# Strassen convolution: partial sums kept in the accumulators, weight sums formed once and stored, VectorE in GpSimd's place

## The chip, the cores and the metric

One core of a Trainium2 chip runs the whole program. The metric is the device time of one execution in microseconds (us). Of the core's engines, TensorE multiplies matrices into eight accumulator banks, VectorE and ScalarE work element by element and can reach those banks, GpSimd works element by element in local memory alone, and SyncE (SP) issues transfers.

## The reference

One decoder step on 2048 prompt tokens and 8 x 16 sample tokens, 2176 in all, 1024 features, fp32 throughout. The change touches only the input side of the first mixer:

```python
def _rmsnorm(x, g):
    y = xf * lax.rsqrt(jnp.mean(xf * xf, axis=-1, keepdims=True) + EPS)
    return (y * g.astype(jnp.float32)).astype(x.dtype)

def _short_conv_mixer(xn, prev, w_in, conv_w, w_out):
    proj = xn @ w_in                                   # 1024 x 4096
    b_gate, c_gate, h, z = jnp.split(proj, 4, axis=-1)
    u = c_gate * h
    up = jnp.concatenate([prev.astype(u.dtype), u], axis=1)
    conv = conv_w[0] * up[:, 0:T]
    for i in range(1, CONV_WIDTH):                     # width 3
        conv = conv + conv_w[i] * up[:, i:i + T]
    y = jax.nn.silu(z) * b_gate * conv
    return y @ w_out, up[:, T:]
...
x = x + _rmsnorm(h, a_norm_post[i])                    # then keys, values,
                                                       # attention, output
```

## The kernel before, in words

The program is a row of phases: convolution (0 to 812 us), output projection of that mixer, keys and values, attention, and the end. Each phase is a block in which every engine has its own instruction list, and the engines wait for each other by semaphores. The lists are written out by hand, so the order on each engine is fixed, and an instruction that waits holds up everything behind it on its engine.

`phase_conv` computes `xn @ w_in`, the gates, the convolution and y. It goes over the tokens in three passes (`PASSES`, line 219: 640, 768 and 768 tokens), each as two halves of 320 or 384 columns. Within a pass it goes over 16 strips: 8 blocks of 128 features (`c`), and for each two strips `m`, of which the first (even n) gives c_gate and h, the second (odd n) z and b_gate. n counts all 48 strips.

A strip is a 2 x 2 block product by the Strassen-Winograd scheme: seven products in place of eight (`A11_B11` to `A22_T4`, line 226). Weights are the A side, tokens the B side. Each product has an inner length of 512, which is 4 blocks of 128, and every fp32 operand is split into a high and a low part, with three matmuls per block (lines 474 to 476): 12 matmuls a product, 84 a strip. The high part is a ScalarE copy into the rounded type (`high_w` line 546, `high_x` line 535), the low part a VectorE subtraction (`low` line 695, `low_x` line 689). Four of the seven weight operands are sums S1 to S4 of quarters of the raw weights; GpSimd forms them for every strip of every pass (`sums`, line 810). Four of the seven token operands are differences T1 to T4, formed once a pass, on GpSimd but for two in pass 0 (`first_differences`, `second_difference`, `third_difference`, lines 827 to 846, and 753 to 758). There is one high and one low buffer for each of the seven operands, so a split for strip n+1 waits for the product of strip n.

Each strip has three accumulator banks, A, B and C, and strips alternate between two sets. Bank A holds P1 (A11 B11), ScalarE copies it out (line 630), and P2 is added to it by TensorE: c11. Bank B holds P5, VectorE adds P1 to it into v (line 770), P6 (S4 B22) is added to it by TensorE, and VectorE adds u2: c12 (lines 788 to 793). Bank C holds the S2 product; VectorE adds P1 into u2 (line 777); the S3 product is added by TensorE and VectorE adds v: c22 (`c22`, line 708); the A22 product is added and VectorE adds P1: c21 (`c21`, line 715). TensorE's order in strip n (lines 502 to 509): A11, S1, the A22 product of strip n-1, S2, A12, S4, S3.

From the four quarters GpSimd forms u = c_gate * h (`set_u`, line 848). ScalarE and VectorE apply the three taps (`keep_and_tap` line 579, `taps` line 721), GpSimd multiplies by silu(z) (`gate`, line 868) and by b_gate (`finish`, line 878), and SP stores y.

The token tiles of 128 rows are normalized: ScalarE squares and sums (`sums_of`), VectorE takes the reciprocal, ScalarE scales (`scale`), TensorE transposes (`turn`), VectorE multiplies by the gain into the stage (`stage`). The five tiles of pass 0 come first; the other twelve are spread over the odd strips, one tile to two strips, in the pass before they are used. Such a tile's scaling is the last ScalarE work of a strip, and its transposes are the first TensorE work of the next (lines 494 and 653). SP's order is in lines 395 to 446: raw weight blocks (512 KB each, two a strip), tiles, y.

## Time and profile before

| | us |
|---|---|
| median of three runs | 2836.79 (2834.07 to 2838.17) |
| profiled execution, its own time | 2833.93 |
| its span, first to last instruction | 2832.2 |
| TensorE busy | 2690.6 (95%) |
| VectorE busy | 1998.5 (71%) |
| ScalarE busy | 1606.5 (57%) |
| GpSimd busy | 1435.6 (51%) |
| mean granted TensorE clock | 0.98 of 2.4 GHz |

The span is the time from the first to the last instruction of the profiled execution; the execution's own time is 1.7 us longer. The table sums all phases. The change concerns the first 812 us, so the views below look at this stretch. In the trace, idle time of an engine is put down to the instruction that released it ("<-"). A matmul's duration is longer than the distance to the next one, as matmuls overlap in the array: for the pace of TensorE one reads the starts.

### The profile page before, as it was taken

To read this page: it belongs to the slowest core of one execution; us is meant where nothing else is said; L and a number is where in the kernel's file an instruction comes from. 1 tells how busy PE (TensorE), PEld (TensorE's weight loads), DVE (VectorE), ACT (ScalarE), POOL (GpSimd) and SP (SyncE) were. 2 spreads that over 40 slices of the span, in tenths; PEclk is the share of its full clock that TensorE was granted. 3 is DMA by queue.
4 is the path that set the end of the run, shared out by engine and by line. 5 is a ranking of instruction groups with operands and counts; after the bars stand their busy time and mean duration, and the time that the engine had idled before them with its cause. 6 is when DMAs were issued, how large, how long until landed. Compare 5 with 4: busy or idle time off the path is not lost. (4 is left out here: it accounts for less than half of the span.)

```text
span 2832.2 us, 44315 instructions
## 1 busy us (share of the span) xinstructions
PE 2690.6 (95%) x15048; PEld 2407.0 (85%) x15048; DVE 1998.5 (71%) x2590; ACT 1606.5 (57%) x3224; POOL 1435.6 (51%) x1251
## 2 busy tenths in 40 slices
PE   5997999799899999999989999999999999989998
PEld 5997999799888888889978988888888888877886
DVE  6777766877754460102248999999999999998775
ACT  5564454444333441111147888888888888875543
POOL 5767655776540021003346777777786768652110
PEclk8998999899999999999999999999999999999999
DMA  3332232133244443434578777767676866757873
GB/s 107 118 99 69 85 110 83 51 113 94 71 146 133 131 147 136 178 114 154 164 218 251 216 230 228 207 216 232 196 242 204 244 208 196 234 180 214 245 227 108
DMA packets 371536, 467.40 MB, mean 165 GB/s; under 512 B 53346, under 2 KB 312546, under 8 KB 365316
## 3 DMA queue, kind: packets, MB, share of 16 engines
q1 hardware_dynamic: 364612, 440.69, 51.4%
q0 software_dynamic: 6720, 24.13, 2.6%
q8 instruction: 110, 1.80, 0.3%
q14 instruction: 94, 0.77, 0.1%
HBM read 340.95 MB, written 123.81 MB: 164 GB/s over the span
## 5 line engine op out<-in xcount | busy, mean ns | idle before, releaser
L2318 POOL TENSOR_TENSOR a_a<-a_a,a_prod 128x512 f32<-128x512 f32 (+3 forms) x640 | 662.0, 1052 | 274.1 <-DVE a_prod L2269 196.9
L474 PE MATMUL c_pc<-c_xh,c_wh 128*128 128x384 f32 (+1 forms) x1344 | 453.3, 337 | 58.3 <-DVE c_sums L706 32.8
L2269 DVE TENSOR_TENSOR_SCAN a_prod<-a_keep,a_prod,a_restart 128x513 f32<-128x513 f32 x384 | 478.4, 1270 | 7.6 <-ACT a_keep L2213 7.0
L476 PE MATMUL c_pc<-c_xh,c_wl 128*128 128x384 f32 (+1 forms) x1344 | 449.2, 334 | 0.0
L475 PE MATMUL c_pc<-c_xl,c_wh 128*128 128x384 f32 (+1 forms) x1344 | 449.2, 334 | 0.0
L2212 ACT ACTIVATE a_a<-a_pz 128x512 f32<-128x512 f32 (+3 forms) x640 | 357.4, 559 | 70.2 <-PE a_pz L2139 48.5
L2279 DVE TENSOR_TENSOR a_atl<-a_pt,a_ath 128x512 fp32r<-128x512 f32 (+3 forms) x640 | 363.4, 600 | 31.9 <-ACT a_ath L2222 28.9
L2222 ACT ACTIVATE a_ath<-a_pt 128x512 fp32r<-128x512 f32 (+3 forms) x640 | 332.9, 559 | 56.9 <-PE a_po L2153 33.3
L2213 ACT ACTIVATE a_keep<-a_pz 128x512 f32<-128x512 f32 (+3 forms) x640 | 361.2, 565 | 0.0
L474 PEld LDWEIGHTS c_pc<-c_xh,c_wh 128*128 128x128 f32 x1344 | 261.5, 195 | 63.9 <-DVE c_sums L706 35.9
L2162 PEld LDWEIGHTS a_pt<-ident_r,a_bits 128*128 128x128 f32 x2176 | 231.0, 141 | 52.1 <-DVE a_atl L2279 8.4
L475 PEld LDWEIGHTS c_pc<-c_xl,c_wh 128*128 128x128 f32 x1344 | 261.3, 194 | 0.0
L476 PEld LDWEIGHTS c_pc<-c_xh,c_wl 128*128 128x128 f32 x1344 | 261.0, 194 | 0.0
L2138 PE MATMUL a_pz<-a_kh,a_q 128*128 128x512 f32 (+3 forms) x640 | 247.5, 390 | 8.5 <-ACT a_keep L2213 6.1
L2151 PE MATMUL a_po<-a_ath,a_v 128*128 128x512 f32 (+3 forms) x640 | 250.0, 394 | 1.9 <-POOL a_v L2329 1.1
L2162 PE MATMUL a_pt<-ident_r,a_bits 128*128 128x128 f32 x2176 | 243.9, 241 | 7.3 <-DVE a_atl L2279 5.0
L699 DVE TENSOR_TENSOR c_wl<-c_s,c_wh 128x512 fp32r<-128x512 f32 x192 | 199.2, 1037 | 69.9 <-ACT c_wh L554 65.1
L2139 PE MATMUL a_pz<-a_kl,a_q 128*128 128x512 f32 (+3 forms) x640 | 234.2, 368 | 0.0
L2153 PE MATMUL a_po<-a_atl,a_v 128*128 128x512 f32 (+3 forms) x640 | 229.3, 367 | 0.0
L554 ACT ACTIVATE c_wh<-c_s 128x512 fp32r<-128x512 f32 x192 | 120.5, 629 | 176.3 <-PE c_pc L476 138.3
L699 DVE TENSOR_TENSOR c_wl<-c_raw,c_wh 128x512 fp32r<-128x512 f32 x144 | 152.7, 1060 | 94.0 <-ACT c_wh L554 92.3
L2263 DVE TENSOR_TENSOR_SCAN a_prod<-a_keep,a_restart 128x128 f32<-128x128 f32 (+3 forms) x256 | 197.3, 807 | 9.5 <-ACT a_keep L2213 8.8
(252 smaller groups left out, 5999.6 us busy)
## 6 DMA issues: line engine op xcount, KB each, us to landing
a_x<-x_d SPq DMA_DIRECT2D x84, 896.0 KB, 7.0
c_raw<-in_a_w_in SPq DMA_DIRECT2D x96, 512.0 KB, 4.1
a_x<-x_d SPq DMA_DIRECT2D x56, 832.0 KB, 5.6
a_kh<-kh_t SPq DMA_DIRECT2D x32, 512.0 KB, 7.1
a_kl<-kl_t SPq DMA_DIRECT2D x32, 512.0 KB, 9.1
x<-f_xn POOLq DMA_DIRECT2D x17, 512.0 KB, 5.2
g_y_in<-sz_t SPq DMA_DIRECT2D x17, 512.0 KB, 8.3
g_x<-x SPq DMA_DIRECT2D x17, 512.0 KB, 4.5
```

The lines of the kernel that those rows point to most:

```text
L474: pe.matmul(o, room.wh[i][:, k, :], x_h, start=fresh and k == 0, stop=False, skip_group_check=True)
L475: pe.matmul(o, room.wh[i][:, k, :], x_l, start=False, stop=False, skip_group_check=True)
L476: mm = pe.matmul(o, room.wl[i][:, k, :], x_h, start=False, stop=k == NH - 1, skip_group_check=True)
L699: dve.tensor_tensor(room.wl[i][:, :, :], room.weights(n, i), room.wh[i][:, :, :].bitcast(F32), ALU.subtract).then_inc(w_lo[i], 1)
L2151: pe.matmul(o, v2[hh][:, kb, :, :], ath[:, b % AS, c0:], start=first, stop=False, skip_group_check=True)
L2162: mm = pe.transpose(pt[:, turn_slot(pr, hh, b), q * P:(q + 1) * P].bitcast(F32R), a_bits[:, unit_slot(hh, u), q, j * P:(j + 1) * P], ident ...
L2212: act.activation(a[:, s, q, 0:w], pz[:, n % ZS, 0:w], ACT.Sigmoid, scale=SCALE)
L2213: act.activation(keep[:, n % KS, 0:w], pz[:, n % ZS, 0:w], ACT.Sigmoid, scale=-SCALE).then_inc(z_used, 1)
L2222: act.activation(ath[:, b % AS, c0:], pt[:, turn_slot(pr, hh, b), c0:], ACT.Copy).then_inc(at_hi, 1)
L2269: dve.tensor_tensor_scan(prod[:, s, 0:w + 1][:, ::-1], keep[:, n % KS, 0:w + 1][:, ::-1], restart[:, 0:1].broadcast_to([P, w + 1]), prod[: ...
L2279: dve.tensor_tensor(atl[:, b % AS, c0:], pt[:, turn_slot(pr, hh, b), c0:], ath[:, b % AS, c0:].bitcast(F32), ALU.subtract).then_inc(at_spl ...
L2318: pool.tensor_tensor(part, part, prod[:, n % PS, after:after + w], ALU.mult).then_inc(weighted, 1)
```

## The change

The passes are 768, 768 and 640 tokens. The first pass has six tiles.

**Accumulators.** ScalarE copies P1 from bank A into bank C (`move_p1`). The S2 product is added there by TensorE, so bank C holds u2 and later, with the A22 product added, c21, without an addition by VectorE. ScalarE copies bank B (P5 alone) and u2 out of the banks (`read_p5`, `read_u2`). c22 is bank C plus P5, c12 bank B plus u2, both on VectorE. At the start TensorE multiplies the identity into both C banks, so that later products add to what stands there.

**Weight sums.** VectorE forms S1 to S4 in pass 0 only (`sum_weights`); SP stores them in DRAM and loads them in passes 1 and 2 (`store_sum`, `load_sum`). The raw block of part 1 is loaded in half there.

**VectorE in GpSimd's place.** All differences of tokens are on VectorE (`difference`), spread over the last strips of the pass before. c21 is multiplied at once: by cg into the first half of u in even strips, into the first half of t in odd ones. GpSimd keeps the second half of u, both multiplications by silu(z), and the last product of the second half.

**Tiles.** ScalarE scales a late tile after the A22 split in the even strip, TensorE transposes it after product A12 of the same strip, and VectorE stages it at that strip's end. In the first pass VectorE scales three of the six tiles, and the order of the start is written anew. The taps are loaded by GpSimd's queue.

The diff, cut to its core:

```diff
-PASSES = [(0, 320), (640, 384), (1408, 384)]
+PASSES = [(0, 384), (768, 384), (1536, 320)]
...
+            def store_sum(n, k):
+                if n < PER_PASS:
+                    sp.wait_ge(summed[k], n + 1)
+                    apart(sp, passed_sp)
+                    sp.dma_start(sum_of(n, k), room.s[k][:, :, :]).then_inc(sum_stored[k], 16)
+
+            def load_sum(n, k):
+                if PER_PASS <= n < NSTRIP:
+                    sp.wait_ge(w_lo[SUMS[k]], n)
+                    sp.wait_ge(sum_stored[k], 16 * PER_PASS)
+                    apart(sp, passed_sp)
+                    sp.dma_start(room.s[k][:, :, :], sum_of(n, k)).then_inc(sum_loaded[k], 16)
...
+                load_sum(n + 1, 2)
+                load_sum(n + 2, 0)
+                if n + 2 < NSTRIP:
+                    free_raw(n, 1)
                     load_raw(n + 2, 1)
...
+                load_sum(n + 2, 1)
                 if n + 3 < NSTRIP:
-                    sp.wait_ge(w_lo[A11_B11], n + 2)
-                    sp.wait_ge(w_lo[A12_B21], n + 2)
-                    sp.wait_ge(summed, 4 * (n + 2))
-                    apart(sp, passed_sp)
+                    free_raw(n + 1, 0)
                     load_raw(n + 3, 0)
+                load_sum(n + 2, 3)
+                for k in (0, 1, 3):
+                    store_sum(n + 2, k)
                 if n == PER_PASS * (NPASS - 1) + 4:
...
-                w, fresh = width(n), i in (A11_B11, S1_T1, S2_T2)
+                w, fresh = width(n), i in (A11_B11, S1_T1)
...
-                elif n >= 2 and i == S2_T2:
-                    pe.wait_ge(c21_read, n - 1)
-                elif i == A12_B21:
-                    pe.wait_ge(p1_read, n + 1)
+                elif i in (S2_T2, A12_B21):
+                    pe.wait_ge(p1_moved, n + 1)
                 elif i == S4_B22:
-                    pe.wait_ge(v_read, n + 1)
...
+            for n in range(2):
+                for k in range(PW_MAX // P):
+                    pe.matmul(pc[:, 3 * n + BANK_C, k * P:(k + 1) * P], ident_r[:, :], ident_r[:, :], start=k == 0,
+                              stop=k == PW_MAX // P - 1, skip_group_check=True)
...
+            for n in range(1, NSTRIP):
                 product(n, A11_B11)
                 product(n, S1_T1)
-                if n:
-                    product(n - 1, A22_T4)
+                product(n - 1, A22_T4)
                 product(n, S2_T2)
                 product(n, A12_B21)
+                if n - 1 in norm_of:
+                    turn(norm_of[n - 1])
...
+            def move_p1(n):
+                act.wait_ge(done[A11_B11], n + 1)
+                wait_past(act, c21_used, n - 1)
+                act.activation(bank(n, BANK_C, width(n)), bank(n, BANK_A, width(n)), ACT.Copy).then_inc(p1_moved, 1)
...
+                wait_past(act, c12_read, n)
+                act.activation(room.u2[:, 0:width(n)], bank(n, BANK_C, width(n)), ACT.Copy).then_inc(u2_read, 1)
...
+                if n:
+                    move_p1(n)
                 high(n + 1, A11_B11)
-                if m == 0 and n:
+                if n and n % 2 == 0:
                     open_gate(n - 1)
-                if m == 0:
+                if n % 2 == 0:
                     prefix(n)
+                if n:
+                    read_p5(n)
                 high(n + 1, S1_T1)
                 high(n, A22_T4)
-                if m == 1:
+                if n - 1 in norm_of:
+                    scale(norm_of[n - 1])
+                if n % 2:
                     keep_and_tap(n)
...
+                read_c11(n)
                 high(n + 1, A12_B21)
+                if n in norm_of:
+                    sums_of(norm_of[n])
                 high(n + 1, S4_B22)
                 high(n + 1, S3_T3)
-                if n in norm_of:
-                    sums_of(norm_of[n])
-                if n - 1 in norm_of:
-                    scale(norm_of[n - 1])
                 if n == LAST:
...
+                if k in (1, 3):
+                    dve.wait_ge(summed[(k - 1) // 2], n + 1)
+                if n:
+                    dve.wait_ge(w_lo[SUMS[k]], n)
+                    dve.wait_ge(sum_stored[k], 16 * n)
+                dve.tensor_tensor(s[k], first, second, op).then_inc(summed[k], 1)
...
             def c22(n):
                 w = width(n)
                 dve.wait_ge(done[S3_T3], n + 1)
-                wait_past(dve, u_set if n % 2 else y_done, 2 * pair(n) + (1 if n % 2 else -1))
-                dve.wait_ge(v_read, n + 1)
-                add(room.sums[:, 1, 0:w], n, BANK_C, room.v[:, 0:w], c22_read)
+                dve.wait_ge(p5_read, n + 1)
+                wait_past(dve, late_y_done if n % 2 else late_u_set, pair(n))
+                dve.tensor_tensor(room.sums[:, n % 2, 0:w], bank(n, BANK_C, w), room.p5[:, n % 2, 0:w], ALU.add)\
+                   .then_inc(c22_read, 1)
 
             def c21(n):
                 w = width(n)
                 dve.wait_ge(done[A22_T4], n + 1)
-                wait_past(dve, u_set if n % 2 else y_done, 2 * (pair(n) + n % 2))
-                add(room.sums[:, 0, 0:w], n, BANK_C, room.p1[:, n % 2, 0:w], c21_read)
+                if n % 2:
+                    dve.wait_ge(half_gated, 2 * pair(n) + 1)
+                    dve.tensor_tensor(room.t[:, 0:w], room.t[:, 0:w], bank(n, BANK_C, w), ALU.mult).then_inc(c21_used, 1)
+                else:
+                    dve.wait_ge(c11_read, n + 1)
+                    wait_past(dve, tapped, pair(n))
...
+            difference(0, S1_T1)
+            sum_weights(0, 0)
+            low(0, S1_T1)
+            sum_weights(0, 1)
+            sum_weights(0, 3)
+            low(0, S4_B22)
+            difference(0, S2_T2)
+            low(0, S2_T2)
+            difference(0, S3_T3)
+            sum_weights(0, 2)
+            for k in (0, 1, 3):
...
             for n in range(NSTRIP):
-                w = width(n)
-                if n:
+                p, turning = n // PER_PASS, n % PER_PASS == PER_PASS - 1 and n != LAST
+                if n and not first_of_pass(n):
                     c22(n - 1)
-                    low(n, S3_T3)
+                low(n, S3_T3)
+                sum_weights(n + 1, 2)
                 low(n + 1, A11_B11)
-                dve.wait_ge(done[S1_T1], n + 1)
-                dve.wait_ge(p1_read, n + 1)
-                wait_past(dve, c22_read, n)
-                add(room.v[:, 0:w], n, BANK_B, room.p1[:, n % 2, 0:w], v_read)
+                if turning:
+                    difference(p + 1, S2_T2)
+                if n - 1 in norm_of:
+                    inverse(norm_of[n - 1])
                 low(n + 1, S1_T1)
                 if n:
                     c21(n - 1)
+                if first_of_pass(n):
+                    difference(p, A22_T4)
                 low(n, A22_T4)
-                dve.wait_ge(done[S2_T2], n + 1)
-                wait_past(dve, c12_read, n)
-                add(room.u2[:, 0:w], n, BANK_C, room.p1[:, n % 2, 0:w], u2_read)
-                low(n + 1, S2_T2)
                 if n % 2:
                     taps(n)
+                if p < NPASS - 1 and n % PER_PASS in (PER_PASS - 3, PER_PASS - 2):
+                    difference(p + 1, S1_T1 if n % PER_PASS == PER_PASS - 3 else S3_T3)
+                low(n + 1, S2_T2)
+                if turning:
+                    c22(n)
                 low(n + 1, A12_B21)
-                if n - 2 in norm_of:
-                    stage(norm_of[n - 2])
+                c12(n)
+                low(n + 1, S4_B22)
...
+                    stage(norm_of[n - 1])
+                for k in (0, 1, 3):
+                    sum_weights(n + 2, k)
...
+            for n in range(NSTRIP):
+                if n % 2 == 0:
+                    set_late_u(n)
+                else:
+                    gate(n, 0)
+                    gate(n, 1)
+                    finish_late(n)
```

## Rows read from the trace of the kernel before

**Rows 1.** The profile's page: busy time and share of the span, instructions.

```profile
PE 2690.6 (95%) x15048; PEld 2407.0 (85%) x15048; DVE 1998.5 (71%) x2590; ACT 1606.5 (57%) x3224; POOL 1435.6 (51%) x1251
```

**Rows 2.** Windows: stretch, length, busy us (instructions) per engine, clock, DMA share, GB/s.

```profile
21.00:55.00 34.00, 17.89 (x86) 16.63 (x85) 27.94 (x29) 13.77 (x19) 18.98 (x8) 0.75 0.23 66
55.00:245.00 190.00, 178.85 (x1228) 176.91 (x1228) 144.44 (x200) 108.39 (x184) 131.49 (x98) 1.00 0.35 100
245.00:295.00 50.00, 32.98 (x164) 31.52 (x163) 42.33 (x32) 20.28 (x29) 39.96 (x19) 0.80 0.17 49
295.00:523.00 228.00, 217.44 (x1232) 215.53 (x1232) 156.25 (x203) 111.39 (x191) 133.12 (x99) 0.97 0.31 91
523.00:571.00 48.00, 33.08 (x167) 32.31 (x166) 41.85 (x33) 20.48 (x31) 37.42 (x18) 0.82 0.19 53
571.00:809.00 238.00, 227.80 (x1280) 225.19 (x1278) 168.50 (x217) 94.60 (x192) 148.00 (x111) 0.98 0.30 91
1500.00:2500.00 1000.00, 996.29 (x6059) 881.28 (x6057) 956.39 (x1265) 864.37 (x1922) 735.15 (x698) 1.00 0.73 221
```

**Rows 3.** Timeline of TensorE: start, duration, instruction [idle before]; two paces.

```profile
129.74 0.31 PE L474 MATMUL c_pc<-c_xh,c_wh 128*128 128x320 f32 x1
...
133.26 0.31 PE L474 MATMUL c_pc<-c_xh,c_wh 128*128 128x320 f32 x1
...
342.41 0.33 PE L474 MATMUL c_pc<-c_xh,c_wh 128*128 128x384 f32 x1
...
349.17 0.33 PE L474 MATMUL c_pc<-c_xh,c_wh 128*128 128x384 f32 x1
```

**Rows 4.** Timeline of TensorE at the start of the first strip.

```profile
21.37 0.64 PE L474 MATMUL c_pc<-c_xh,c_wh 128*128 128x320 f32 x1
...
31.52 0.63 PE L474 MATMUL c_pc<-c_xh,c_wh 128*128 128x320 f32 x1 [7.16 <-DVE c_xl L692]
```

**Rows 5.** TensorE at a turned tile: timeline; waits (total, times, longest), 55 to 245.

```profile
82.25 0.87 PE L486 MATMUL c_pt<-ident_r,c_norm_bits 128*128 128x128 f32 x8 [1.76 <-ACT c_norm L532]
...
PE c_pt L486 <- ACT c_norm L532: 10.6, 6, 1.8
```

**Rows 6.** Timeline of TensorE at the first change of pass.

```profile
263.13 0.64 PE L474 MATMUL c_pc<-c_xh,c_wh 128*128 128x320 f32 x1 [3.91 <-DVE c_u L706]
...
282.68 0.63 PE L474 MATMUL c_pc<-c_xh,c_wh 128*128 128x320 f32 x1 [10.56 <-DVE c_sums L706]
```

**Rows 7.** Timeline in pass 2: TensorE, and ScalarE ten us before.

```profile
713.26 0.69 PE L474 MATMUL c_pc<-c_xh,c_wh 128*128 128x384 f32 x1 [3.93 <-DVE c_sums L706]
...
703.04 0.20 ACT L592 ACTIVATE c_edge<-c_u 128x2 f32<-128x2 f32 x1 [4.54 <-POOL c_u L865]
```

**Rows 8.** Timeline at 243 us: GpSimd (POOL), then VectorE (DVE).

```profile
243.56 3.53 POOL L831 TENSOR_TENSOR c_t<-c_stage 128x1536 f32<-128x1536 f32 x1
...
243.60 4.03 DVE L699 TENSOR_TENSOR c_wl<-c_s,c_wh 128x512 fp32r<-128x512 f32 x1 [0.18 <-ACT c_wh L554]
```

**Rows 9.** VectorE by line: duration ns min/median/max; last: busy us, mean ns.

```profile
L699 DVE TENSOR_TENSOR c_wl<-c_s,c_wh x192: 673/903/4028, 26.7 to 791.6; 128x512 fp32r<-128x512 f32 x192
...
L753 DVE TENSOR_TENSOR c_t<-c_stage x1: 1493/1493/1493, 23.7 to 23.7; 128x1280 f32<-128x1280 f32 x1
...
L706 DVE TENSOR_TENSOR c_sums<-c_pc,c_p 128x384 f32<-128x384 f32 x32 | 17.7, 552 | 13.0 <-PE c_pc L476 12.9
```

**Rows 10.** GpSimd by line, 0 to 815 us: busy us, mean ns, idle.

```profile
L822 POOL TENSOR_TENSOR c_s<-c_raw 128x512 f32<-128x512 f32 x48 | 74.5, 1553 | 51.6 <-DVE c_wl L699 51.6
...
L886 POOL TENSOR_TENSOR c_t<-c_t,c_sums 128x384 f32<-128x384 f32 x32 | 42.3, 1340 | 3.4 <-DVE c_sums L706 2.3
```

**Rows 11.** ScalarE by line, 0 to 815 us: busy us, mean ns, idle.

```profile
L554 ACT ACTIVATE c_wh<-c_s 128x512 fp32r<-128x512 f32 x192 | 120.5, 629 | 176.3 <-PE c_pc L476 138.3 <-POOL c_s L817 36.4 <-POOL c_s L825 1.0
...
L630 ACT ACTIVATE c_p<-c_pc 128x384 f32<-128x384 f32 x32 | 15.6, 487 | 44.4 <-PE c_pc L476 44.4
```

**Rows 12.** Loads of raw weights, all 96 of 512 KB.

```profile
DMA to landing us min/median/max: 3.8/4.1/9.7
```

383 lines of the change are left out of this document (190 added, 193 removed).

## The prediction

> **What bounds the kernel now.** I read the page first, then the busy time by stretch, then the gaps ahead of TensorE, then the engines that filled those gaps. TensorE is busy 95% of the whole span [rows 1], and after the convolution it is full: 996 us of 1000 in the attention stretch [rows 2]. So the span shortens by whatever the convolution phase shortens, one for one. The change touches only this phase.
>
> Inside the phase I need TensorE's pace without waits. Between two matmuls of 320 columns lie (133.26 - 129.74)/24 = 0.1467 us, between two of 384 columns (349.17 - 342.41)/39 = 0.1733 us [rows 3]. A strip is 7 products of 12 matmuls, so 12.3 or 14.6 us. All 4032 matmuls need 1344 x 0.1467 + 2688 x 0.1733 = 663 us; from the first product at 21.4 [rows 4] to the last near 809 the phase takes 788. The loss is 125 us. The same subtraction by stretch, the lengths from [rows 2]:
> - First strip, 21 to 55: 34 us for 72 matmuls (10.6): 23 lost, TensorE waiting for sums, differences and splits of the first tiles; one such wait is 7.16 us [rows 4].
> - Strips 1 to 14: 190 for 172.5: 17.5 lost. Six of these strips begin with eight transposes that wait 1.76 us for ScalarE's scaling and take 0.87 themselves [rows 5]: 6 x 2.63 = 15.8, nearly all.
> - First change of pass, 245 to 295: 50 for 26.9: 23 lost, in gaps of 3.91 and 10.56 us behind VectorE [rows 6], at a mean clock of 0.80.
> - Strips 17 to 30: 228 for 203.8: 24 lost: six more transposes, 15.8, and 8 us at the lower clock (0.97 for the stretch).
> - Second change of pass, 523 to 571: 48 for 29.1: 19 lost.
> - The rest: 238 for 220.4: 17.6 lost, half of it in gaps such as the 3.93 us behind a VectorE sum [rows 7].
>
> Behind most of these gaps stands GpSimd. In [rows 8] a VectorE subtraction of 0.68 us lasts 4.03 us because a GpSimd operation of 3.53 us began just before it. Over the phase this form has minimum 0.673 and median 0.903 us [rows 9], although its work is always the same. The Trainium skill, page "SBUF — State Buffer", section "Who interferes with whom", says that an operation of VectorE with two SBUF inputs and one of GpSimd that reads SBUF take turns on a shared port, the later one blocked fully; by that rule the trace agrees.
>
> **The change, part by part.**
>
> *Sums of weights leave GpSimd.* 48 x 4 operations of about 1.55 us vanish there [rows 10]. Pass 0 forms 16 x 4 on VectorE; the nearest row is the split of the same shape, 0.68 us, 0.60 from start to start. The other 128 become loads. In steady work VectorE then has, per pair of wide strips of pass 0: 14 splits x 0.6 = 8.4, 8 sums x 0.6 = 4.8, 6 reads of accumulators x 0.47 = 2.8 (0.552 each by duration [rows 9]), two taps 1.8 (768/1280 of the 1.49 in [rows 9]), staging a tile 1.2: 19 us of 29.1. Later passes have 14.2. Against it stand the two additions (v and u2) that go to ScalarE as copies, and the c21 addition, which merges with the product that GpSimd did. GpSimd keeps one product for u and three for the gate per pair, about 5 us at the 1.34 of [rows 10]; all its operations overlap VectorE for at most those 5 us, where they now do for most of the phase.
>
> The point that decides is where c22 lands. TensorE needs it before product A22 of the next strip, two products (4.16 us) after the strip's end. VectorE reaches it after the split of S4, a staging in even strips and three sums. In an odd strip ScalarE's tile sums delay the S4 split to about 15.5 us from the strip's start; three sums bring it to 17.5, c22 to 18.0, the limit is 14.56 + 4.16 = 18.7. In an even strip it comes at 18.4 against 19.8. So it fits with about 1 us, uncontended. That is my thinnest cover.
>
> *Copies on ScalarE.* Two more per strip; one writes an accumulator, which no row shows. Bounds: 0.487 us, the copy out of the accumulators, and 0.629, a copy of 512 columns [rows 11]; I take 0.5. Below nothing it can't be, as it is added work. 96 copies are 48 us, beside other work: ScalarE is busy 108 of 190 us in [rows 2]. Move of P1: ready 2.6 us into the strip, S2 wants it at 6.2. The copy of u2 is ready at 8.8, S3 wants it at 12.5. Hidden. The Trainium skill, page "ScalarE: Activation LUTs", section "Step-by-step: what each stage is for", calls a write to PSUM faster than one to SBUF; no row here shows it, and the sum would not change.
>
> *Transposes.* The scaling moves from the end of a strip to before its middle, the transposes of that tile to after product A12 one strip later. 1.76 us of waiting goes each time, the 0.87 stays, and there are 11 late tiles instead of 12: 31.6 - 9.6 = 22 us saved. Late next: nothing, the scaled tile is ready about 3 us ahead. ScalarE's square for the following tile moves ahead of the splits of S4 and S3; those wait for TensorE anyway, and the delay is in the c22 reckoning above.
>
> *Changes of pass.* The differences move from GpSimd to VectorE: 1.49 us at 1280 elements [rows 9], so 1.79 at 1536, for the 3.53 on GpSimd [rows 8]. S1 and S3 are formed in the two strips before, where VectorE has no more sums. Left: S2's difference in the last strip, which pushes c21, hence the taps and with them ScalarE's u2 copy, and A22's difference in the next, behind which the same copy queues: 0.5 and 3 us by adding durations, and GpSimd's gate may block VectorE for 1.3 twice. I take 5 us each, bounds 1 and 12. Saved: 42 - 10 = 32.
>
> *Pass 2.* The late u came from GpSimd behind its weight sums: ScalarE idled 4.54 us for it [rows 7]. VectorE now writes half of u directly. 17.6 falls to about 3 (the eight edge transposes stay, c22 is near its limit beside the border weights). Saved: 14.6. Strips of this pass are 320 wide now and pass 0 is 384: the total stays 663.
>
> *Lower clock in pass 1.* It sat behind the 2.6 us gaps; with them gone I keep 2 of the 8 us: 6 saved.
>
> *Start.* Six tiles instead of five; VectorE scales three and does all differences and sums in one row. Adding durations in queue order, TensorE's first product starts at 20.7 (now 21.4), the S1 product at 34.5 behind difference, sum, split, S4 at 40, S2 at 45, S3 at 51, strip 1 at 55, and c22 of strip 0, behind strip 2's sums, holds A22 for 3.8 us. Net 2 us dearer than now, bounds -8 and +12.
>
> *Queues.* SP gets 64 stores in pass 0 and 128 loads of 256 KB later, and 256 KB less in each of 32 raw loads. It now waits for every sum in order. The raw load of part 1 goes out at about 7.7 us of a strip and is wanted 7.8 us later; landing is 4.1 us at 512 KB [rows 12]. Stored sums are wanted a strip later. Traffic grows from 100 to about 150 GB/s, below the 221 of [rows 2]. Free, with 3.7 us of cover; the taps' loads go to GpSimd's queue, and are wanted at 67 us. At the end VectorE multiplies the last accumulator into t itself, and GpSimd's closing product, 1.34 by [rows 10], goes from the path: 1.3 saved.
>
> **The sum.** -22 - 32 - 14.6 - 6 + 2 - 1.3 = -74; I add 8 us for VectorE blocked by what is left on GpSimd (24 pairs, 5 us of overlap each; bounds 0 and 24): -66. The profiled run took 2833.9, its span 2832.2; the median of runs is 2.9 above it. 2833.9 - 66 = 2768, on the scale of the median 2771.
>
> **The rivals.**
> - *VectorE is late in pass 0* (c22 misses its limit). For it: 1 us of cover, and splits whose median is 0.9 rather than 0.67 now. With 11 operations 0.3 us dearer, c22 comes 2 to 3 us late in each of 15 strips: 35 us back, 2806. Against: GpSimd is quiet for most of a pair. Chance 0.12. The Trainium skill, page "Perfetto Trace Analysis", section "Optimizing Scalar/DVE Operations", advises to move work off a saturated DVE, if need be to GPSIMD, and adds that between those two it might not help: the first half speaks for this rival, the lock in [rows 8] for the second half.
> - *Slower than now*: the same place, if the sums in front of c22 cost over 66/15 = 4.4 us a strip beyond cover. Every one of the 11 operations would have to last 1.35 us, twice 0.68: 11 x 0.67 = 7.4, less cover 1, 6.4 x 15 = 96 us back, 2867. It decides from 1.17 us an operation. Chance 0.03.
> - *SP's order starves a load*: a raw block lands 9.7 us after issue at worst now; if each of 15 strips waited 2 us, with slow matmuls after, 40 back: 2811. Chance 0.06.
> - *The covers hold better*: no blocking, start 8 us better: 2753. Chance 0.12.
> - The forecast, 2771: 0.67.
>
> **How the numbers follow.** The range leaves out the slower case, half of the two with 2806 and 2811, and the lower part of the better one: 2753 to 2804. 0.2% is 6 us, about what can be told here. Faster 0.95, same 0.02, slower 0.03.
>
> **What would show it.** Strips of 14.6 us in mid-pass with the transposes inside; no TensorE wait for the scaling; VectorE splits near a median of 0.68; changes of pass of 32 to 35 us for two strips; strip 1 starting near 55. It would be wrong if TensorE waits behind c22 in pass 0, if raw loads end waits, or if the changes of pass still cost 20 us.

## The result and the profile after

The changed kernel takes 2763.3 us (median; 2762.5 to 2764.7) against 2835.4 (2834.0 to 2838.2) for the kernel before: ratio 0.9745, 95% interval 0.9728 to 0.9762, so 72 us faster. The forecast was 2771. The profiled run of after took 2762.5, its span is 2760.8. Its page, busy time, share of the span and instructions:

```profile
PE 2678.2 (97%) x15054; PEld 2398.8 (87%) x15054; DVE 1914.0 (69%) x2571; ACT 1639.1 (59%) x3315; POOL 1040.3 (38%) x1004
```

Its windows (columns as in [rows 2]), cut where its own stretches end:

```profile
22.00:58.00 36.00, 23.69 (x97) 21.67 (x96) 28.95 (x33) 15.69 (x21) 0.00 (x0) 0.77 0.26 88
58.00:270.00 212.00, 211.18 (x1227) 210.53 (x1228) 164.26 (x237) 125.16 (x217) 36.77 (x28) 0.99 0.54 170
270.00:305.00 35.00, 30.82 (x169) 30.18 (x168) 31.51 (x32) 21.68 (x34) 6.15 (x4) 0.95 0.41 121
305.00:513.00 208.00, 208.00 (x1219) 207.83 (x1218) 118.43 (x172) 118.01 (x213) 32.73 (x28) 1.00 0.51 150
513.00:558.00 45.00, 41.14 (x253) 40.88 (x252) 37.85 (x46) 26.89 (x50) 7.74 (x7) 0.96 0.42 126
558.00:733.00 175.00, 175.00 (x1195) 174.44 (x1194) 113.66 (x170) 96.35 (x207) 36.39 (x37) 1.00 0.55 170
```

Against [rows 1] GpSimd lost 395 us of work. Against [rows 2] TensorE is now busy for 211 of 212 us in strips 1 to 14, for all 208 in strips 17 to 30 and all 175 in the last pass. What is left shows in TensorE's waits, 0 to 745 us (engine, tile, line <- releaser: us in total, times, longest):

```profile
PE c_pc L505 <- DVE c_xl L795: 14.0, 3, 5.7
PE c_pc L505 <- ACT c_u L616: 8.0, 2, 4.2
...
PE c_pc L505 <- DVE c_sums L812: 0.8, 1, 0.8
```

The 14 us belong to the start and the 8 to the changes of pass. The scaling of token tiles, 10.6 us in [rows 5], is gone, and c22 ends one short wait.

The prediction's own subtraction (length of the strips less their matmuls at 0.1467 or 0.1733 us), cut at strip boundaries, gives the loss of each stretch. Every kernel is in the table; "median" is against the 2763.3 of after, for b_turn against the 2835.0 measured beside it. "Changes" are strips 15, 16 and 31 to 33.

| kernel | strip 0 | 1-14 | 17-30 | changes | 34-47 | sum | median |
|---|---|---|---|---|---|---|---|
| before | 22.8 | 17.2 | 23.1 | 24.0 + 19.4 | 16.9 | 123.5 | |
| after | 23.8 | 7.9 | 4.1 | 6.0 + 6.0 | 1.1 | 48.9 | |
| b_turn | 20.6 | 21.7 | 4.8 | 22.4 + 21.9 | 15.2 | 106.6 | -11.9 |
| late_turn | 22.7 | 26.8 | 18.8 | 6.3 + 6.0 | 1.1 | 81.6 | +31.6 |
| gp_sums | 21.9 | 6.9 | 4.6 | 5.8 + 7.0 | 1.1 | 47.2 | -2.6 |
| gp_all | 21.0 | 5.5 | 5.0 | 11.7 + 11.7 | 9.1 | 64.0 | +15.0 |
| no_store | 23.8 | 7.9 | 4.0 | 9.0 + 9.7 | 8.1 | 62.5 | +14.4 |
| gp_diff | 22.6 | 8.5 | 5.0 | 8.3 + 8.0 | 1.1 | 53.5 | +4.7 |
| gp_both | 21.4 | 6.5 | 4.9 | 18.3 + 15.6 | 8.6 | 75.3 | +24.4 |
| gp_load | 23.6 | 13.2 | 4.1 | 9.7 + 9.9 | 1.1 | 61.5 | +13.4 |
| c22_delay | 23.7 | 25.9 | 4.4 | 6.6 + 6.9 | 1.1 | 68.4 | +18.2 |
| dve_reads | 26.3 | 8.0 | 5.1 | 9.8 + 8.5 | 1.1 | 58.8 | +6.9 |
| u2_start | 20.2 | 7.8 | 6.4 | 0.3 + 4.6 | 1.1 | 40.3 | -9.1 |
| best | 21.2 | 5.5 | 4.1 | 0.3 + 0.5 | 1.1 | 32.6 | -15.9 |

Each row is read from one profiled execution. The intervals of gp_sums, gp_diff, dve_reads and u2_start overlap that of after, so for these four the table carries the reading and not the median.

The convolution phase lost 75 us of idle time, the span only 71.4. From the end of the last product to the end of the span before takes 2023.7 us, after 2027.4, and the other kernels, whose later phases are the same, between 2024.2 (gp_diff) and 2030.8 (gp_load). The missing 4 us lie inside that scatter; b_turn, with the later phases of before, has 2029.2. I give them no cause.

### The profile page after: what moved, and what is told of

The parts are those of the page before. It is cut to its first block and busy times, and to the rows that moved or that the text cites. A ratio compares the mean times of both kernels' runs of the same rounds, so it can differ in the third digit from the quotient of the medians.

```text
span 2760.8 us, 44501 instructions
## 1 busy us (share of the span) xinstructions
PE 2678.2 (97%) x15054; PEld 2398.8 (87%) x15054; DVE 1914.0 (69%) x2571; ACT 1639.1 (59%) x3315; POOL 1040.3 (38%) x1004
## 5 line engine op out<-in xcount | busy, mean ns | idle before, releaser
L505 PE MATMUL c_pc<-c_xh,c_wh 128*128 128x384 f32 (+1 forms) x1344 | 446.4, 332 | 24.9 <-DVE c_xl L795 14.0
L507 PE MATMUL c_pc<-c_xh,c_wl 128*128 128x384 f32 (+1 forms) x1344 | 443.5, 330 | 0.0
L506 PE MATMUL c_pc<-c_xl,c_wh 128*128 128x384 f32 (+1 forms) x1344 | 443.4, 330 | 0.0
L505 PEld LDWEIGHTS c_pc<-c_xh,c_wh 128*128 128x128 f32 x1344 | 256.2, 191 | 28.3 <-DVE c_xl L795 9.9
L802 DVE TENSOR_TENSOR c_wl<-c_s,c_wh 128x512 fp32r<-128x512 f32 x192 | 148.7, 775 | 77.1 <-ACT c_wh L599 74.2
L1566 DVE CAST v_hi<-v_pg 128x384 fp32r<-128x384 f32 (+1 forms) x40 | 24.5, 612 | 228.3 <-ACT v_full L1512 227.8
L959 POOL TENSOR_TENSOR c_t<-c_t,c_sz 128x384 f32<-128x384 f32 (+1 forms) x48 | 57.3, 1194 | 329.6 <-ACT c_sz L626 175.0
```

The costliest lines, as they stand in the source:

```text
L505: pe.matmul(o, room.wh[i][:, k, :], x_h, start=fresh and k == 0, stop=False, skip_group_check=True)
L506: pe.matmul(o, room.wh[i][:, k, :], x_l, start=False, stop=False, skip_group_check=True)
L507: mm = pe.matmul(o, room.wl[i][:, k, :], x_h, start=False, stop=k == NH - 1, skip_group_check=True)
```

## The experiments

### The placing of scaling and transposes

**late_turn**: after, with this undone.

```diff
 for n in range(1, NSTRIP):
+    if n - 2 in norm_of:
+        turn(norm_of[n - 2])
     product(n, A11_B11)
...
     product(n, A12_B21)
-    if n - 1 in norm_of:
-        turn(norm_of[n - 1])
```

ScalarE's `scale` and `sums_of` go behind `high(n + 1, S3_T3)`, VectorE's `stage` behind `low(n, A22_T4)`.

> The kernel after, with the scaling and the transposes of the later token tiles placed as before: transposes at the start of strip n for the tile of n-2, the scaling last in ScalarE's strip. Theory: PE waits for the scaling again, and each of the 12 turned tiles outside the changes of pass costs 2.6 us in place of 0.7 us: +20 to +26 us. Rival: the shorter ScalarE and GpSimd queues of the kernel after would hide it anyway, and it costs under 6 us.

Measured +31.6 us, more than either (and for eleven tiles, not the twelve I had counted). TensorE's waits in the phase:

```profile
PE c_pt L520 <- ACT c_norm L573: 19.3, 11, 1.8
```

Windows (columns as in [rows 2]) around one turned tile, whose transposes end at 123.8:

```profile
119.00:123.80 4.80, 3.04 (x22) 2.72 (x20) 4.01 (x7) 2.30 (x3) 0.21 (x1) 1.00 1.04 339
...
123.80:126.00 2.20, 2.20 (x10) 2.20 (x9) 1.52 (x2) 0.00 (x0) 1.17 (x1) 0.56 0.42 158
126.00:128.00 2.00, 2.00 (x9) 2.00 (x9) 0.00 (x0) 0.24 (x1) 0.00 (x0) 0.63 0.35 131
128.00:130.00 2.00, 2.00 (x13) 2.00 (x12) 0.69 (x1) 0.91 (x3) 0.00 (x0) 1.00 0.00 0
```

The wait of 1.76 us is back, eleven times. After seven of the eleven TensorE is busy without a pause, yet for some 4 us its granted clock is 0.56 to 0.63, near its lower level of 1.2 GHz, and it completes 10 and 9 matmuls where 13 fit. That costs 1.65 us in each of seven strips. After the other four the clock holds, as behind the same wait at 190.1:

```profile
190.00:196.00 6.00, 5.93 (x38) 5.93 (x39) 3.33 (x5) 1.81 (x5) 1.39 (x1) 1.00 0.41 152
```

With the 2.64 us of wait and transposes in place of 0.72 eleven times it makes 7 x 1.65 + 11 x 1.92 = 32.7 us, the whole difference in the table. With 0.72 us of transposes and no wait, as after has them, the clock stays at 1.00.

**b_turn**: the same move made in the kernel before (there `inverse` and `stage` move as well, to where after has them).

> The kernel before, with only the scaling and the transposes of the later token tiles moved to where the kernel after has them. Theory: the wait of 1.76 us at a turned tile goes, and 11 to 12 of them give 1.9 us each: -18 to -26 us against before. Rival: before's fuller ScalarE and GpSimd make the scaling late at its new place too: 0 to -8 us.

-11.9 us, between the two, and the table says why. In strips 17 to 30 (384 columns) the loss falls from 23.1 to 4.8, as the theory has it. In strips 1 to 14 (320 columns, 12.3 us) it rises from 17.2 to 21.7, and not for the rival's reason: the scaling is not late, c22 is. TensorE's waits from 54 to 248 us:

```profile
PE c_pc L474 <- DVE c_sums L706: 12.6, 7, 1.9
```

What makes c22 late is read backwards from it. GpSimd, ScalarE and VectorE ahead of one such wait (TensorE goes on at 126.80):

```profile
117.92 0.88 POOL L865 TENSOR_TENSOR c_u<-c_sums,c_cg 128x320 f32<-128x320 f32 x1
...
118.83 0.20 ACT L590 ACTIVATE c_carry<-c_u 128x2 f32<-128x2 f32 x1 [3.86 <-POOL c_u L865]
...
120.31 0.69 DVE L699 TENSOR_TENSOR c_wl<-c_s,c_wh 128x512 fp32r<-128x512 f32 x1 [3.10 <-ACT c_wh L554]
120.92 2.72 DVE L727 SCALAR_TENSOR_TENSOR c_t<-c_u,c_taps,c_t 128x640 f32<-128x640 f32 x2
123.57 1.78 DVE L699 TENSOR_TENSOR c_wl<-c_raw,c_wh 128x512 fp32r<-128x512 f32 x1
...
126.27 0.48 DVE L706 TENSOR_TENSOR c_sums<-c_pc,c_v 128x320 f32<-128x320 f32 x1
```

From 120.3 us until c22 VectorE has no idle time, so ScalarE's copies for S4 and S3, done at 124.8, do not hold it up. The delay is older. GpSimd reaches its product for u at 117.9, behind its four weight sums, although the c21 that it needs was there at 115.5; in the kernel before, GpSimd waits for c21 at this place:

```profile
116.51 0.88 POOL L865 TENSOR_TENSOR c_u<-c_sums,c_cg 128x320 f32<-128x320 f32 x1 [1.03 <-DVE c_sums L706]
```

ScalarE's part of the taps waits 3.86 us for that product, the copy for S2 queues behind, and VectorE idles 3.10 us for the copy. Then two taps take 2.72 us (1.80 in the kernel before) and a split 1.78 (0.68), while GpSimd forms the next sums beside them. The square of the next tile and its table load, 2.7 us that now stand ahead of the copies for S4 and S3, are not the cause: before the last of these waits, at 236.9, ScalarE squares no tile, and product A22 waits the same 1.94 us. Two of the six waits of 1.94 us are also followed by the lower clock, here in strips of 320 columns:

```profile
98.50:102.00 3.50, 3.50 (x15) 3.50 (x14) 3.20 (x6) 1.69 (x3) 3.50 (x3) 0.51 0.37 110
```

The move thus removes one wait of TensorE and, where a strip lasts 12.3 us, creates another through GpSimd's full queue; strips of 384 columns cover it. After has such strips in pass 0, and GpSimd forms no sums there. gp_sums below has the sums on GpSimd in wide strips and stays covered; no run turns tiles in narrow strips with GpSimd free of the sums, so that the width was needed is not shown.

### VectorE's cover, and what GpSimd takes from it

**c22_delay**: three operations ahead of c22.

```diff
+                if 2 < n < PER_PASS - 1:
+                    for _ in range(3):
+                        dve.wait_ge(idled, idles[0])
+                        dve.tensor_tensor(room.idle[:, :], room.idle[:, :], room.idle[:, :], ALU.mult).then_inc(idled, 1)
+                        idles[0] += 1
                 if n and not first_of_pass(n):
                     c22(n - 1)
```

> The kernel after, with three multiplications of VectorE's own tile (128x384) directly ahead of the addition for c22 in strips 3 to 14; some 2 us each time, and no result depends on them. It measures the cover that the forecast called its thinnest, about 1 us (0.45 us in strip 8 and 0.7 us in strip 7 by the trace of after). Theory: the addition is held in place by ScalarE's copy of S4's weights, for which VectorE idles just before, so nothing absorbs a delay behind that point, and 12 strips lose 1.3 to 1.6 us each: +14 to +20 us. Rival: the chain is elastic, the slack elsewhere in VectorE's strip takes it up: under +4 us.

+18.2 us: the theory. VectorE's timeline in after, strip 8:

```profile
165.49 0.69 DVE L802 TENSOR_TENSOR c_wl<-c_s,c_wh 128x512 fp32r<-128x512 f32 x1 [1.54 <-ACT c_wh L599]
...
166.97 0.69 DVE L790 TENSOR_TENSOR c_s<-c_s,c_raw 128x512 f32<-128x512 f32 x1 [0.19 <-issue]
...
168.46 0.55 DVE L812 TENSOR_TENSOR c_sums<-c_pc,c_p 128x384 f32<-128x384 f32 x1
```

VectorE and TensorE in the same strip of c22_delay:

```profile
175.90 1.74 DVE L898 TENSOR_TENSOR c_idle<-c_idle 128x384 f32<-128x384 f32 x3
177.55 0.55 DVE L814 TENSOR_TENSOR c_sums<-c_pc,c_p 128x384 f32<-128x384 f32 x1
...
178.16 0.44 PE L507 MATMUL c_pc<-c_xh,c_wh 128*128 128x384 f32 x1 [1.13 <-DVE c_sums L814]
```

The three take 1.65 us from start to start, and strips grow by 1.16 us (odd) and 1.43 us (even). So the cover of c22 is 0.2 to 0.5 us by this difference, thinner than forecast. It is not VectorE's load that makes it so: VectorE idles 1.54 us for ScalarE just before. What counts is the chain from ScalarE's copy through split, three sums and addition. The next run puts work elsewhere in VectorE's strip:

**dve_reads**: after, with `read_p5` and `read_u2` as `dve.tensor_copy` in VectorE's queue, ahead of S1's split and behind A22's.

```diff
-                act.activation(room.p5[:, n % 2, 0:width(n)], bank(n, BANK_B, width(n)), ACT.Copy).then_inc(p5_read, 1)
+                dve.tensor_copy(room.p5[:, n % 2, 0:width(n)], bank(n, BANK_B, width(n))).then_inc(p5_read, 1)
```

> The kernel after, with P5 and u2 copied out of the accumulators by VectorE instead of ScalarE. It moves 2 x 0.49 us from ScalarE to VectorE in each strip, and u2's copy stands behind c_wl's split of A22 in VectorE's queue. Theory: VectorE at some 12.5 us of 14.6 still holds mid-pass, and CC22's cover shrinks but mostly holds: 0 to +10 us, most of it in pass 2 and at the changes of pass. Rival: with two more links on VectorE, S4 or S3 waits in every strip, 0.5 us or more each: +25 us or more.

+6.9 us, inside the theory's range. One microsecond more of VectorE in each strip costs nothing in mid-pass (8.0, 5.1 and 1.1 us lost in strips 1 to 14, 17 to 30 and 34 to 47 against 7.9, 4.1 and 1.1 in after; the 1.0 more in the second is all in strip 17, right behind the change); the cost lies in the start and the changes of pass. The same edit takes as much off ScalarE, so this is not VectorE's added load alone.

**gp_load**: `load_port(k)` is k multiplications of `room.idle` by itself, each waiting for the one before.

```diff
                 if n % 2 == 0:
                     set_late_u(n)
+                    load_port(5)
                 else:
...
                     finish_late(n)
+                    load_port(6)
```

> The kernel after, with GpSimd multiplying a tile of its own by itself (128x384, f32), five times after each gating step of an even strip and six times after those of an odd one, some 6 to 8 us of each strip. Nothing waits for these multiplications and every result stays what it was. Theory of the forecast's term of +8 us: a running GpSimd operation stretches VectorE's, whoever waits for what. Then the median of VectorE's splits of the sums (L802, c_wl<-c_s: 0.69 us in the kernel after) goes toward the 0.90 us of before, CC22's cover of about 1 us (0.5 to 1.4 us in strips 7 and 8) is used up, and the conv phase grows by 0.5 to 1 us in each strip of pass 0 at least: +10 to +40 us. Rival: what cost time before was the dependency (ScalarE's copy waited for a sum that GpSimd had not finished), and the load alone costs under 5 us, with the splits' median under 0.75 us.

+13.4 us: the number lies in the theory's range, but neither reading holds as it was put. VectorE's splits by line (ns min/median/max) in after:

```profile
L802 DVE TENSOR_TENSOR c_wl<-c_s,c_wh x192: 674/691/1533, 32.4 to 719.2; 128x512 fp32r<-128x512 f32 x192
L802 DVE TENSOR_TENSOR c_wl<-c_raw,c_wh x144: 675/692/1508, 18.4 to 724.5; 128x512 fp32r<-128x512 f32 x144
```

In gp_load:

```profile
L804 DVE TENSOR_TENSOR c_wl<-c_s,c_wh x192: 672/692/1527, 32.9 to 732.3; 128x512 fp32r<-128x512 f32 x192
L804 DVE TENSOR_TENSOR c_wl<-c_raw,c_wh x144: 674/914/1517, 18.9 to 737.6; 128x512 fp32r<-128x512 f32 x144
```

Its timeline, GpSimd and VectorE:

```profile
174.22 1.02 POOL L961 TENSOR_TENSOR c_t<-c_t,c_sz 128x384 f32<-128x384 f32 x1 [5.81 <-ACT c_sz L633]
...
176.62 3.74 POOL L981 TENSOR_TENSOR c_idle<-c_idle 128x384 f32<-128x384 f32 x3
...
172.30 0.55 DVE L814 TENSOR_TENSOR c_sums<-c_pc,c_p 128x384 f32<-128x384 f32 x1
...
175.78 1.43 DVE L804 TENSOR_TENSOR c_wl<-c_s,c_wh 128x512 fp32r<-128x512 f32 x1
177.13 0.54 DVE L822 TENSOR_TENSOR c_t<-c_t,c_pc 128x384 f32<-128x384 f32 x1
```

The load does stretch splits. The median of the form that the theory named (c_wl<-c_s) stays at 0.69 us, but its mean rises from 0.78 to 0.88; the median of the other goes from 0.69 to 0.91 us. An addition that reads the accumulators keeps its 0.54 us while GpSimd multiplies. (The Trainium skill, page "SBUF — State Buffer", section "Who interferes with whom", names two SBUF inputs as what makes VectorE take turns with GpSimd; the trace agrees.) But from strip 2 to 13 this costs 0.5 us in all; the rest falls in strips 1, 14, 15 and the changes of pass. The reason for the 0.5 lies in the place of the load: GpSimd idles 5.81 us up to 174.2, and in that time the thin chain runs, S4's split to c22, 169.4 to 172.9. In the strips of pass 0 up to 12 at most 0.8 us of GpSimd's work stands beside that chain, and none in the odd ones. So the load stood mostly where VectorE had idle time, and what a full load would cost beside that chain, with its 0.2 to 0.5 us of cover, this run does not show.

### Who forms the sums

**gp_sums** (pass 0), **gp_all** (all strips, no copies in DRAM): GpSimd forms the sums, between its gates. **no_store**: VectorE, all strips. gp_all and no_store load the raw blocks whole in every pass.

```diff
-                dve.tensor_tensor(s[k], first, second, op).then_inc(summed[k], 1)
+                pool.tensor_tensor(s[k], first, second, op).then_inc(summed[k], 1)
```

That line is gp_sums and gp_all; gp_all and no_store have this one:

```diff
-                if n >= PER_PASS:
+                if n >= NSTRIP:
                     return
```

> The kernel after, with the sums of weights of pass 0 formed on GpSimd (each 1.3 us there against 0.7 to 0.8 us on VectorE), stored and loaded again as after. Theory: mid-pass the move of the sums earned nothing, because before already ran its mid-pass strips at PE's pace save at the turned tiles; so pass 0 keeps 14.6 us a strip, with up to 0.3 us more where a sum comes late, and the whole stays within -2 to +6 us, most of it in the start, where sums on VectorE and on GpSimd cost different amounts. Rival: GpSimd's sums come late or slow VectorE in each strip, 1 to 3 us in each of 16 strips: +16 to +48 us.

-2.6 us: moving the sums to VectorE in pass 0 earned nothing, and 1.9 us less is lost in the start with GpSimd beside it; the intervals (0.9716 to 0.9749, and after's) overlap.

> The kernel after, with the sums of weights formed on GpSimd in all 48 strips, as before, and no copy of them in DRAM; the quarters' differences, gates and copies stay as after. Theory: mid-pass 0 again; at the two changes of pass GpSimd's sums stand in their own queue and no longer in that of the differences, so the S3 waits stay near 4 us each, and pass 2 (12.35 us a strip, VectorE's shortest) loses up to 0.5 us a strip: +2 to +12 us against the kernel after. Rival: the gain came from the sums' copies, and this goes back by 25 us or more toward the kernel before.

+15.0 us, a little over the upper end of the theory. Against gp_sums, which differs from it only in forming the sums once, it is 17.6.

> The kernel after, with VectorE forming the sums of weights in all 48 strips, and neither stores of them nor loads: the raw quarters are loaded whole in every pass. It adds 4 x 0.75 = 3 us of VectorE's time to each strip of passes 1 and 2. Theory: VectorE has some 11.5 us of work in a strip of 14.6, so pass 1 holds; in pass 2 3 us more on 12.35 us of PE leaves it near full, and at the changes of pass the sums stand before the differences: +3 to +20 us. Rival (sums once and kept are worth nothing here): within 2 us; rival (VectorE becomes the bound): passes 1 and 2 go to 15.5 us or more a strip, +40 us or more.

+14.4 us, inside the theory's range. Both kernels lose it at the same places: 11 and 7 us more at the changes, 8 and 7 in the last pass, 1 us at most in strips 17 to 30. TensorE's waits from 564 to 752 us in no_store:

```profile
PE c_pc L505 <- DVE c_sums L811: 5.4, 5, 1.4
```

In gp_all the same wait comes to 5.7 us in four times, the longest 2.0, but in another way. In no_store three sums stand ahead of c22 in VectorE's queue. In gp_all none does; there GpSimd's sums run beside VectorE's split and beside the border weights' subtraction (L214), which both kernels have ahead of c22 in these strips. VectorE in gp_all, then in no_store:

```profile
669.12 1.51 DVE L801 TENSOR_TENSOR c_wl<-c_s,c_wh 128x512 fp32r<-128x512 f32 x1
670.55 2.30 DVE L214 TENSOR_TENSOR b_xh<-f_raw,b_xh 128x1024 fp32r<-128x1024 f32 x1
...
666.75 0.67 DVE L801 TENSOR_TENSOR c_wl<-c_s,c_wh 128x512 fp32r<-128x512 f32 x1
...
670.04 1.22 DVE L214 TENSOR_TENSOR b_xh<-f_raw,b_xh 128x1024 fp32r<-128x1024 f32 x1
```

So here the stretching by GpSimd does cost time: these two operations on the way to c22 last 1.9 us longer. Forming the sums once is worth 14 us with VectorE and 18 with GpSimd; which engine forms them, next to nothing.

### The changes of pass

**gp_diff**: the edit of `difference` for passes 1 and 2.

```diff
-                dve.tensor_tensor(out, first, second, ALU.subtract).then_inc(t_set[order.index(i)], 1)
+                pool.tensor_tensor(out, first, second, ALU.subtract).then_inc(t_set[order.index(i)], 1)
```

GpSimd forms S1's behind the gates of strip 13 of the pass, S3's in strip 14, S2's ahead of the gates of strip 15, A22's behind them.

> The kernel after, with the four differences of quarters for passes 1 and 2 formed on GpSimd (3.5 us each there, 1.75 us on VectorE), in the same strips as after; the differences of pass 0 stay on VectorE. Theory: the gain at the changes of pass came from the differences' engine as well as from their early place; the first two still fit ahead, S2's difference ahead of the gates and A22's behind them come 3 to 6 us later than now, and block VectorE's splits meanwhile: +8 to +22 us in all, every one of them in strips 14 to 17 and 31 to 33. Rival: the early place alone did it, and the engine is worth nothing: under 4 us.

+4.7 us, 4.3 of it at the changes by the table: about half the lower end of the theory, and just over the rival's 4. Alone, the engine is worth little.

**gp_both**: gp_all and gp_diff together.

> The kernel after with the division of labour of before: GpSimd forms the sums of weights in all 48 strips (the edit of gp_all) and the four differences of quarters for passes 1 and 2 (the edit of gp_diff). The partial sums in the accumulators, VectorE's products for u and t, and the early transposes stay as after. Apart, the two edits cost 15.0 and 4.7 us. Theory: at the changes of pass GpSimd's sums and differences stand in each other's way, 14 us of differences in the queue of a strip and a half beside 5 to 6 us of sums a strip, so together they cost more than the 20 us of the sum: +25 to +40 us, the excess over 20 all in strips 13 to 17 and 29 to 33, which would account for most of the loss there in the kernel before. Rival: the costs only add, as they sit at different places: +16 to +23 us, and the rest of before's loss at the changes of pass came from its longer chains of partial sums through VectorE and GpSimd.

+24.4 us, under the theory's lower end by less than the noise and just over the rival's upper end. The table decides it better than the median: at the changes gp_all adds 11.4 and gp_diff 4.3, together 15.7; gp_both adds 21.9. The excess of 6 us is there, but smaller than I thought. Timelines of GpSimd and, last row, TensorE:

```profile
289.30 2.80 POOL L988 TENSOR_TENSOR c_s<-c_raw 128x512 f32<-128x512 f32 x1
...
296.66 2.65 POOL L988 TENSOR_TENSOR c_s<-c_raw,c_s 128x512 f32<-128x512 f32 x1 [2.86 <-DVE c_wl L801]
...
304.83 3.86 POOL L972 TENSOR_TENSOR c_stage<-c_stage 128x1536 f32<-128x1536 f32 x1
...
310.72 0.69 PE L505 MATMUL c_pc<-c_xh,c_wh 128*128 128x384 f32 x1 [10.11 <-ACT c_u L616]
```

A22's difference starts at 304.8 behind sums that wait themselves, and S3 waits 10.1 us, like the product in [rows 6]. Of the 31.4 us between before and after at the changes gp_both takes back 21.9, and of the 15.8 in the last pass 7.5. The rest, 9.5 and 8.3, would by elimination belong to the additions that the accumulators now make, to VectorE's products for u and t and to the order of the widths; no kernel here undid those, so that is argued and not shown.

**u2_start** takes away what was left. In after the timelines of VectorE, ScalarE and TensorE show at the first change:

```profile
293.26 2.56 DVE L795 TENSOR_TENSOR c_xl<-c_stage,c_xh 128x1536 fp32r<-128x1536 f32 x1
...
297.42 1.74 DVE L773 TENSOR_TENSOR c_stage<-c_stage 128x1536 f32<-128x1536 f32 x1
...
299.28 1.48 ACT L585 ACTIVATE c_xh<-c_stage 128x1536 fp32r<-128x1536 f32 x1 [6.39 <-DVE c_stage L773]
300.67 0.47 ACT L616 ACTIVATE c_u<-c_pc 128x384 f32<-128x384 f32 x1
...
301.19 0.69 PE L505 MATMUL c_pc<-c_xh,c_wh 128*128 128x384 f32 x1 [4.18 <-ACT c_u L616]
```

ScalarE stands 6.39 us in front of A22's quarter while the 0.47 us copy of u2, which S3 needs, queues behind it.

```diff
                 high(n + 1, S1_T1)
+                if n and first_of_pass(n):
+                    read_u2(n)
                 high(n, A22_T4)
```

The new order of the start is told in its expectation; the difference for S2 also goes ahead of S4's split.

> The kernel after with two changes of order. First, in the first strip of passes 1 and 2 ScalarE copies u2 before it copies A22's weights and quarter, which wait for VectorE's difference. Second, at the start VectorE forms the first weight sum before it stages tiles 4 and 5, the second before S1's split, and S3's weight sum before the difference that S3 needs. Theory: PE's two waits of 4.2 and 4.0 us at S3 in those strips come from the copy's place in ScalarE's queue, and go, since A22's product stands two products (4 us) after S3: -6 to -9 us; the start gives 1 to 4 us, since S1 waits 5.8 us and the sum of 0.7 us stands in front of it: -7 to -13 us in all. Rival: S3 then waits for its own quarter (VectorE's difference and split) and keeps 3 us or more: -1 to -4 us.

-9.1 us. Strip 0 loses 3.6 us less. S3's waits are gone; in their place A22 waits 2.09 and 2.39 us one strip later, for c22 (the expectation of best has them as 2.26 and 2.53) (strip 17 stands in the column 17-30). TensorE's timeline:

```profile
302.47 0.44 PE L505 MATMUL c_pc<-c_xh,c_wh 128*128 128x384 f32 x1 [2.09 <-DVE c_sums L814]
```

**best** joins gp_sums and u2_start and reorders VectorE in those strips.

```diff
                 low(n, S3_T3)
+                if n and first_of_pass(n):
+                    difference(p, A22_T4)
...
                 low(n + 1, S2_T2)
-                if turning:
+                if turning or n and first_of_pass(n):
                     c22(n)
                 low(n + 1, A12_B21)
```

> The kernel after, with the edits of gp_sums and u2_start as far as they go together (weight sums of pass 0 on GpSimd, stored as after; u2 copied before A22's operands in the first strips of passes 1 and 2), and two more on VectorE there: A22's difference stands directly behind S3's split, and c22 of that strip ahead of A12's split instead of at the head of the next strip. Theory: what is left of the changes of pass in u2_start, waits of 2.26 and 2.53 us at A22 for c22, goes; the start gains what gp_sums and u2_start gained, of which 2 us is the same: -14 to -20 us against the kernel after. Rival: A22 then waits for another, or the start's gains are one and the same: -9 to -12 us.

-15.9 us: 2747.5 us (ratio to before 0.9690, interval 0.9674 to 0.9706), faster than both kernels. Its windows at the two changes:

```profile
266.00:296.00 30.00, 30.00 (x174) 29.70 (x173) 27.19 (x26) 20.23 (x30) 6.18 (x4) 1.00 0.37 112
...
504.00:543.00 39.00, 39.00 (x249) 38.86 (x249) 35.00 (x43) 26.45 (x49) 9.46 (x7) 1.00 0.47 138
```

TensorE is busy throughout, at full clock. Of the 32.6 us that best still loses, 21 are in strip 0.

## Why the prediction was right, and where not

- **Transposes (-22) and lower clock (-6).** Together 28; strips 1 to 14 and 17 to 30 lose 28.3 us less. Right in sum. But undoing the move costs 33.6 in these strips and making it alone brings 13.8. My bookkeeping held the two terms apart, while in late_turn the lower clock comes back with the wait. And "late next: nothing" holds for after but not for the move as such: b_turn shows A22 late next in strips of 320 columns, behind GpSimd's sums. The prediction dealt with the widths in one sentence, as leaving the total at 663, and reckoned c22 for wide strips with GpSimd quiet. That fits the kernel after; what the step does in other strips it did not ask.
- **Changes of pass (-32).** 31.4 measured; 6.0 us stays each time where I took 5. The mechanism of what stays, u2's copy queued behind A22's difference, is as written. The differences' new engine, with which I argued, is worth 4 us; the sums' leaving the queue is worth more (11.4), and 9.5 us of the gain no run traces to a cause.
- **Pass 2 (-14.6).** 15.8 in strips 34 to 47, 1.1 stays instead of 3. About half of it comes from sums no longer formed there (7 to 8 us by gp_all and no_store). This step named the sums only as what stood ahead of u, and put the gain down to VectorE writing half of u; no run tests that, and 8 us stay without a shown cause.
- **Start (+2).** The loss of strip 0 grew by 1.0, and strip 1 started at 57.9, not 55. The first product came at 21.6, not 20.7: ScalarE waited 2.4 and 2.1 us for the third and fourth tile's load (row below). S1, S4, S2 and S3 started at 35.6, 40.9, 45.9 and 52.8 where I had 34.5, 40, 45 and 51. c22 of strip 0 held A22 for 0.8 instead of 3.8 us.

```profile
10.07 1.06 ACT L565 ACTIVATE c_norm<-c_x_first 128x1024 f32<-128x1024 f32 x1 [2.36 <-DMA c_x_first<-in_x_prompt]
```

- **VectorE blocked by GpSimd (+8).** This term failed, and the forecast lies above the result by about its size: without it the sum is -74, and the phase shortened by 75. (The span shortened by less, as the later phases took nearly 4 us more.) The median of the splits is near 0.69 us as expected. Beside the chain from S4's split to c22 no GpSimd operation runs in strips 1 to 13 of after, and even gp_load's additional 296 us of them cost 0.5 us in strips 2 to 13. A stretched operation stands in the rows of the first change, a split of 2.56 us in place of 1.75; the changes of pass were already charged by themselves. I had charged durations on VectorE to the end of the kernel where idle time takes them up. That the lock can cost time on the chain to c22 is seen in gp_all.
- **c22.** "About 1 us" was 0.2 to 0.5. It held, so the forecast did; the rival at 2806 was nearer than its 0.12 suggests, since more than 0.5 us behind ScalarE's copy would have begun it. The three sums took 2.4 us from their start to c22's where I had reckoned some 2.
- **Copies on ScalarE.** 0.5 was taken. P5's takes 486 ns and u2's 491; the copy that no row had shown, from accumulator to accumulator, takes 475:

```profile
L606 ACT ACTIVATE c_pc<-c_pc 128x384 f32<-128x384 f32 x32 | 15.2, 475 | 43.6 <-PE c_pc L507 43.6
```

By the rule of the Trainium skill that the prediction cited from page "ScalarE: Activation LUTs", section "Step-by-step: what each stage is for" (a write to PSUM is the faster one) the trace agrees, by 11 to 16 ns.

- **Queues.** SP starved nothing: no wait of TensorE in the convolution ends with a load, and the loads that ScalarE waited for at the start are those of token tiles.
- **End (-1.3).** Not to be told apart: the later phases differ by more.

## What to carry to other kernels

Measure cover on the one chain that leads to the waiting product, not by an engine's load: here a delay of 1.65 us at one place cost 1.2 to 1.4 us a strip, and a microsecond of work elsewhere on the same engine nothing in mid-pass. Taking a wait away is worth more than its length where the clock falls behind it, and less where another queue had lived on that pause, as GpSimd's in b_turn; so try such a move in every strip width it runs in, and read the new wait back through all engines before naming its cause. In a strip that differs from the others, look at what queues behind its one long wait: moving a copy of 0.47 us ahead of it removed two waits of 4 us, though two of 2.1 and 2.4 us came in their place until VectorE's queue was reordered too.

## What I had not expected of the hardware

- TensorE's granted clock fell to near its lower level after seven of eleven equal pauses (1.76 us of waiting, then 0.87 us of transposes, late_turn, 384 columns), and after two of six waits of 1.94 us in strips of 320 columns (b_turn). In the kernel before it kept 1.00 after the six waits of 1.76 us in strips of 320 columns [rows 2]. So neither the length of the wait nor the width decides it alone; I have no explanation.
- VectorE idles 0.19 us between two weight sums of which the second needs the first (rows of strip 8 above): 0.88 us from start to start, not the 0.60 that I had added. It is not so for every such pair: the three operations in c22_delay also wait for one another, and their three times 0.55 to 0.56 us take 1.74 in all, which leaves less than 0.04 us of idle time between two. What makes the difference is open.
